# Twelve weight pages of block one multiplied in high and low halves, a first sum of squares that needs no constants from memory, and a fill moved

## The reference

```python
h = rms_norm(x, norm1_g[l])                     # divides by the root of the mean square over 1024
proj = h @ w_in[l]
p_rwkv, p_sb, q_mem, gate_logits = jnp.split(proj, cut, axis=-1)
...
q, k, v = jnp.split(p, 3, axis=-1)              # stick-breaking branch: v is h @ 512 columns
...
kv = rms_norm(mem, mem_g) @ w_kv                # memory branch
mk, mv = jnp.split(kv, 2, axis=-1)              # 512 columns of keys, 512 of values
```

## Time and profile before

| | us |
|---|---|
| median of 3 runs | 1359.57 |
| the profiled execution | 1355.61 |
| its span in the trace | 1353.8 |
| PE busy | 1259.5 (93%) |
| DVE busy | 818.7 (60%) |
| ACT busy | 680.1 (50%) |
| POOL busy | 571.1 (42%) |

### The profile page before, as it was taken

The page is one execution under the profiler, slowest core; times in us unless marked ns, Lnnn a source line. Parts: engine busy times, 40 slices in busy tenths (PEclk is TensorE's granted clock), DMA queues, the critical chain, the costliest instruction groups (busy, mean ns, idle before and its releaser), DMA issues.

```text
span 1353.8 us, 21687 instructions
## 1 busy us (share of the span) xinstructions
PE 1259.5 (93%) x8350; PEld 904.4 (67%) x8350; DVE 818.7 (60%) x1859; ACT 680.1 (50%) x1508; POOL 571.1 (42%) x385
## 2 busy tenths in 40 slices
PE   9999999999999999999999998888989888888786
PEld 7988988989999999987896443333434333433232
DVE  5876003473478763467247777666677676667755
ACT  4832233745676665653335654445554445554544
POOL 1100043327888888720014444444444444444342
PEclk9999999999999999999999999999999999999999
DMA  7433232335555555555739999999999999999997
GB/s 267 139 112 97 95 109 79 127 137 167 178 177 182 187 187 187 171 191 200 261 122 423 421 421 422 421 422 421 421 422 421 421 422 421 422 421 421 422 421 300
DMA packets 67935, 381.02 MB, mean 281 GB/s; under 512 B 7552, under 2 KB 7552, under 8 KB 35200
## 3 DMA queue, kind: packets, MB, share of 16 engines
q0 software_dynamic: 37296, 268.45, 47.8%
q1 hardware_dynamic: 29664, 107.84, 23.8%
q10 hardware_dynamic: 880, 3.41, 0.6%
HBM read 378.63 MB, written 1.05 MB: 280 GB/s over the span
## 4 chain that ended last, share of the span: by engine, by line
PE 59%; DMA 27%; ACT 6%; DVE 5%; issue 2%; POOL 1%; SPq 0%; POOLq 0%; DVEq 0%; ACTq 0%
DMA arena_block<-in_experts,arena_block 26%; PE bank L467 23%; PE bank L1092 10%; PE bank L503 5%; PE bank L521 3%; PE bank L465 2%; DVE arena_block L2480 2%; PE bank L1016 2%; PE bank L889 2%; PE bank L1116 1%; PE bank L485 1%; DMA const<-in_const 1%; ACT arena_block L1702 1%; PE bank L1026 1%; PE bank L566 1%
## 5 line engine op out<-in xcount | busy, mean ns | idle before, releaser
L1092 PE MATMUL bank<-arena_block 128*128 128x512 f32 x1012 | 486.5, 611 | 82.1 <-ACT arena_block L1702 80.5
L2617 POOL DMA_INDIRECT arena_block<-in_experts,arena_block x253 | 273.7, 1082 | 466.4 <-PE bank L1092 331.5
L2480 DVE SCALAR_TENSOR_TENSOR arena_block<-arena_block 128x1024 f32<-128x1024 f32 x256 | 314.0, 1227 | 188.9 <-DMA arena_block<-in_experts,arena_block 184.9
L1092 PEld LDWEIGHTS bank<-arena_block 128*128 128x128 f32 x1012 | 178.4, 190 | 350.1 <-ACT arena_block L1702 212.2
L2594 POOL TENSOR_TENSOR w_lo<-ring,w_hi 128x1024 fp32r<-128x1024 f32 x100 | 242.8, 2450 | 85.0 <-ACT w_hi L1200 84.7
L1696 ACT ACTIVATE arena_block<-arena_block 128x1 f32<-128x1 f32 x256 | 75.1, 294 | 279.7 <-DVE arena_block L2480 279.4
L1200 ACT ACTIVATE w_hi<-ring 128x1024 fp32r<-128x1024 f32 x119 | 125.2, 1053 | 51.9 <-PE bank L503 28.8
L467 PE MATMUL bank<-x_hi,w_hi 128*128 128x256 f32 x384 | 109.0, 284 | 0.0
L467 PE MATMUL bank<-x_hi,w_lo 128*128 128x256 f32 x384 | 108.7, 283 | 0.0
L467 PE MATMUL bank<-x_lo,w_hi 128*128 128x256 f32 x384 | 108.7, 283 | 0.0
L1702 ACT ACTIVATE arena_block<-const,arena_block 128x128 f32<-128x128 f32 x256 | 102.7, 401 | 8.3
(11 more groups left out here) (537 smaller groups left out, 2418.0 us busy)
## 6 DMA issues: line engine op xcount, KB each, us to landing
ring<-in_pages SPq DMA_DIRECT2D x175, 512.0 KB, 3.4
wq_pages<-in_pages SPq DMA_DIRECT2D x16, 512.0 KB, 4.6
arena_block<-in_experts,arena_block POOLq DMA_INDIRECT x259, 14.9
arena_block<-in_pages SPq DMA_DIRECT2D x8, 512.0 KB, 6.9
arena_mix<-in_memT ACTq DMA_DIRECT2D x1, 1024.0 KB, 8.9
arena_block<-in_subkT ACTq DMA_DIRECT2D x1, 1024.0 KB, 6.3
const<-in_const SPq DMA_DIRECT2D x1, 974.5 KB, 13.1
out_tok<-arena_block SPq DMA_DIRECT2D x3, 256.0 KB, 7.4
```

The lines of the kernel that those rows point to most:

```text
L1092: last = mm(bank[2 * tt + j][:, :], diag[:, slot, :], uv[slot][:, D + j * 512:D + (j + 1) * 512], start=start, stop=stop)
L2480: stt(uv[s][:, 0:D], uv[s][:, 0:D], 1.0, htok[:, tt, :], ALU.mult, ALU.mult, accum_out=e_act[:, s:s + 1])\
L2617: nc.gpsimd.indirect_dma_start(out=uv[slot], out_offset=None, in_=A["experts"], in_offset=bass.IndirectOffsetOnAxis(ap=eidx[:, n:n + 1], a ...
```

## The change

Pages 26 to 37 become split pages (`SPLIT_END` from 26 to 38), so `sbv`, `mk` and `mv` are three fp32r products where they were one float32 product. ScalarE makes their high halves (`a_high(26)` to `a_high(37)`) and VectorE their low ones (`a_low(26)` to `a_low(37)`), in places of the arena that are free then (`value_hi`, `early_hi`, `mem_hi`). The normed memory is split as well (`memn_hi` on ScalarE, `memn_lo` on VectorE). Low halves of pages up to 37 are counted by a semaphore of their own, `lo_first`. The four squares of `sbq`, `sbk`, `mq` and `mk` on VectorE move behind the last page of `mv`. The fill of `DT` moves behind `a_low(26)`. The first sum of squares uses a tile of ones that VectorE writes at the start and stands behind page 1, outside any page; the wait for `const` moves to behind page 5.

```diff
-SHIFTED, ROWED, FIRST_SPLIT, SHIFTED_END, FROM_KEYS, SPLIT_END = 14, 5, 7, 17, 19, 26
+SHIFTED, ROWED, FIRST_SPLIT, SHIFTED_END, FROM_KEYS, SPLIT_END = 14, 5, 7, 17, 19, 38
...
         def page_ready(page):
-            if page in NTH:
-                pe.wait_ge(S("lo_ready"), NTH[page])
+            if page in FIRSTS:
+                pe.wait_ge(S("lo_first"), NTH[page])
+            elif page in NTH:
+                pe.wait_ge(S("lo_ready"), NTH[page] - LATER)
...
-        linear("in_a", xg, part=(2, 1), between=first_norm)
-        a_page(3, 3)
+        pe.wait_ge(S("warm_tile"), 2)
+        pe.wait_ge(S("sq_tree"), 3)
+        mm(bank[4][:, 0:T], hn[:, 1, 0:P], norm_at[0][0][:, 0, :], start=True, stop=True).then_inc(S("norm_sum"), 1)
+        a_page(2, 4)
+        pe.wait_ge(S("const_in"), 16)
...
-        linear("sbv", hn, by_token=True, part=(1, 1))
+        linear("sbv", hn_hi_first, hn_lo_early, by_token=True, part=(1, 1))
...
-        pe.wait_ge(S("norm_out"), 2)
-        linear("mk", memn, part=(0, 1))
+        pe.wait_ge(S("b_dve"), B_DVE["memn_split"])
+        linear("mk", memn_hi, memn_lo, part=(0, 1))
...
-        linear("mv", memn, by_token=True)
-        pe.wait_ge(S("hn_high"), 1)
+        linear("mv", memn_hi, memn_lo, by_token=True)
+        pe.wait_ge(S("b_act"), B_ACT["hn_high"])
...
         take("sbv", flat(sbv), part=(0, 1))
+        a_high(28)
         act.wait_ge(S("b_dve"), B_DVE["inv3"])
...
+        act.wait_ge(S("norm_out"), 2)
+        A_(memn_hi, memn, ACT.Copy).then_inc(S("b_act"), 1)
         take("sbv", flat(sbv), part=(1, 1))
+        a_high(29)
...
         v.memset(hn[:, 0, :], 0.0).then_inc(S("warm_tile"), 1)
+        v.memset(hn[:, 1, 0:P], 1.0).then_inc(S("warm_tile"), 1)
...
         near_cross(2)
-        dve.wait_ge(S("in_a_copy"), SHIFTED_END - SHIFTED)
-        v.memset(DT, 0.0)
...
         pairs_read(5)
-        dve.wait_ge(S("in_a_copy"), N_IN_A - SHIFTED - 4)
-        tt_(sq_of["sbq"], sbq, sbq, ALU.mult)
+        a_low(26)
+        v.memset(DT, 0.0)
         pairs_read(6)
+        a_low(27)
...
+        a_low(28)
+        dve.wait_ge(S("b_act"), B_ACT["memn_high"])
+        tt_(memn_lo, memn, memn_hi.bitcast(F32), ALU.subtract).then_inc(S("b_dve"), 1)
+        a_low(29)
```

More of the change, by code:

```diff
@@ L50 @@
 SPLIT = IN_PLACE + [p for p in range(SPLIT0, N_PAGES) if p not in WHOLE]
+LATER = len(FIRSTS)
 LAST_GATE = EARLY[15]
@@ L273, in build @@
     hn_hi_first = typed(9728, "hn_hi_first", KT)
+    value_hi = [typed(start, f"value_hi{i}", 4).rearrange("p a b -> p (a b)") for i, start in enumerate((W0 + 15640, W0 + 16664))]
+    mem_hi = [value_hi[0], typed(4096, "mem_hi", 4).rearrange("p a b -> p (a b)")]
+    memn_hi = typed(2048, "memn_hi", KT)
+    lo_space = nc.sbuf_tensor("memn_lo", [P, KT, T], F32R)
+    memn_lo = lo_space.__enter__()[:, :, :]
+    lo_space.__exit__(None, None, None)
     y_hi, y_lo = typed(18944, "y_hi", 8), typed(11776, "y_lo", 8)
@@ L286, in high_room @@
         if page in FIRSTS:
-            return first_hi[page % SLOTS if page < PAGE0["in_a"] + SHIFTED_END else page % 2]
+            if page < PAGE0["in_a"] + SHIFTED_END:
+                return first_hi[page % SLOTS]
+            if page < PAGE0["sbv"]:
+                return first_hi[page % 2]
+            if page < PAGE0["mk"]:
+                return value_hi[page % 2]
+            return early_hi[page % 2] if page < PAGE0["mv"] else mem_hi[page % 2]
         if page in EARLY:
@@ L402, in _ @@
             if page - SLOTS in NTH and page - SLOTS not in IN_PLACE:
-                sp.wait_ge(S("lo_ready"), NTH[page - SLOTS])
+                sp.wait_ge(S("lo_ready"), NTH[page - SLOTS] - LATER)
             else:
@@ L525, in norm_sum @@
         def norm_sum(i):
-            if i < 2:
-                pe.wait_ge(S("sq_tree"), 3 * i + 3)
+            if i == 1:
+                pe.wait_ge(S("sq_tree"), 6)
             else:
@@ L700, in _ @@
                 pe.wait_ge(S("norm_out"), 1)
-                linear("sbv", hn, by_token=True, part=(0, 1))
+                linear("sbv", hn_hi_first, hn_lo_early, by_token=True, part=(0, 1))
             near_dd(lv)
             pairs(2 * lv + 1)
-        linear("sbv", hn, by_token=True, part=(1, 1))
+        linear("sbv", hn_hi_first, hn_lo_early, by_token=True, part=(1, 1))
         pe.wait_ge(S("b_dve"), B_DVE["inv3"])
@@ L710, in _ @@
         last.then_inc(S("b_pe"), 1)
-        linear("sbv", hn, by_token=True, part=(2, 1))
+        linear("sbv", hn_hi_first, hn_lo_early, by_token=True, part=(2, 1))
         pe.wait_ge(S("b_act"), B_ACT["pp32"])
@@ L719, in _ @@
         last.then_inc(S("b_pe"), 1)
-        linear("sbv", hn, by_token=True, part=(3, 1))
+        linear("sbv", hn_hi_first, hn_lo_early, by_token=True, part=(3, 1))
         pe.wait_ge(S("b_dve"), B_DVE["dd32"])
@@ L731, in _ @@
         last.then_inc(S("b_pe"), 1)
-        linear("mk", memn, part=(1, 1))
+        linear("mk", memn_hi, memn_lo, part=(1, 1))
         pe.wait_ge(S("b_dve"), B_DVE["pairs7"])
         chunk_g(0)
-        linear("mk", memn, part=(2, 1))
+        linear("mk", memn_hi, memn_lo, part=(2, 1))
         pe.wait_ge(S("b_act"), B_ACT["dd64"])
         chunk_u(0)
-        linear("mk", memn, part=(3, 1))
+        linear("mk", memn_hi, memn_lo, part=(3, 1))
         chunk_y(0)
@@ L1346, in _ @@
         act.wait_ge(S("norm_out"), 1)
-        A_(hn_hi, hn, ACT.Copy).then_inc(S("hn_high"), 1)
+        A_(hn_hi, hn, ACT.Copy).then_inc(S("b_act"), 1)
         take("mk", mk, part=(0, 1))
+        a_high(32)
         act.wait_ge(S("b_pe"), B_PE["dd64"])
@@ L1368, in _ @@
         take("mk", mk, part=(1, 1))
+        a_high(33)
         g_copy(0)
         take("mk", mk, part=(2, 1))
+        a_high(34)
         u_copy(0)
         take("mk", mk, part=(3, 1))
+        a_high(35)
         y_copy(0)
-        take("mv", flat(mv), part=(0, 2))
+        take("mv", flat(mv), part=(0, 1))
+        a_high(36)
+        take("mv", flat(mv), part=(1, 1))
+        a_high(37)
         high(EARLY[0])
@@ L1867, in a_low @@
             dve.wait_ge(S("hi_ready"), NTH[page])
-            tt_(ring_lo[:, page % SLOTS, :], ring[:, page % SLOTS, :], high_room(page).bitcast(F32), ALU.subtract).then_inc(S("lo_ready"), 1)
+            tt_(ring_lo[:, page % SLOTS, :], ring[:, page % SLOTS, :], high_room(page).bitcast(F32), ALU.subtract).then_inc(S("lo_first"), 1)
         norm_mean(0)
@@ L1994, in _ @@
         step(tt_(col[:, 25:26], V("mem_q_g"), V("mem_k_g"), ALU.mult))
+        for b in range(30, 36):
+            a_low(b)
         dve.wait_ge(S("b_pe"), B_PE["state"])
@@ L1997, in _ @@
         tt_(S1, two(bank[4][:, 0:T], 64), fac.broadcast_to([P, 4, 64]), ALU.mult).then_inc(S("b_dve"), 1)
-        dve.wait_ge(S("mk_out"), N_MK)
+        a_low(36)
+        a_low(37)
+        dve.wait_ge(S("mv_out"), N_MV)
+        tt_(sq_of["sbq"], sbq, sbq, ALU.mult)
+        tt_(sq_of["sbk"], sbk, sbk, ALU.mult)
+        tt_(sq_of["mq"], mq, mq, ALU.mult)
         tt_(sq_of["mk"], mk, mk, ALU.mult).then_inc(S("b_dve"), 1)
```

14 lines of the change are left out of this document (5 added, 9 removed).

## The result

| | before | after |
|---|---|---|
| median of 7 runs each, us | 1358.63 (1354.34 to 1362.05) | 1366.72 (1364.78 to 1368.86) |
| the profiled execution, us | 1355.61 | 1366.72 |
| its span, us | 1353.8 | 1364.9 |

The ratio of the runs is 1.0057, with a 95% interval of 1.0038 to 1.0075: some 8 us slower. The two profiled executions differ by 11.1 us. The forecast was +9.7 us, between the two.

The account below looks back on a forecast made before the run. Block one was taken to be bound by TensorE's own time. Terms +13.0 (by-token pages), -2.1 (`mk`) and -1.2 (first sum) gave +9.7 us, on the median 1359.57 forecast as 1369.3; own range 1365 to 1376, overall 1352 to 1379.

Parts of the forecast that it names:

- By-token pages: `sbv` and `mv`: 48 instructions a page instead of 32, 0.109 us each, held by weight loads; +13.0 us together.
- `mk`: Four by-feature pages of the memory's keys, split: 3.05 us each, 12.2 against 14.32 us, so -2.1 us.
- First sum: Start of the kernel: the ones product moves behind page 1, page 5 starts at 24.8 instead of 26.0 us; -1.2 us.
- Halves at no cost: VectorE and ScalarE make the new halves before their pages are due, `a_low(26)` and `a_low(28)` being tightest; cost 0.
- Fill and squares: On VectorE: moving the `DT` fill gives nothing; the four squares are due over 20 us behind `mv`; 0.
- Not in the sum: TensorE waits in the first 215 us for nothing the profile shows: read as 0.9 us, given no term.
- The median: The summed +9.7 us was put on the median of the runs, 1359.57, giving 1369.3 us, 0.7% slower.
- slower by over 0.5%: Whole kernel: outcome given 0.75, 0.55 from the forecast and late halves, 0.20 from narrow products at float32's rate.
- Loads of a reduced type: Rival, by-token pages: loads hidden, 128-column products follow at 0.066 us; -6.8 us in all, 1352.8 us; 20%.
- A narrow product: Rival, by-token pages: a narrow fp32r product streams at float32's rate, 0.227 us each; +55 us, 1415 us; 20%.
- Halves were not late: Rival: TensorE waits for VectorE's halves at two to four new pages, 1.2 to 2 us each; +4, 1373 us; 10%.

Follow-up runs that it names:

- two_products: Changed kernel without the third product (low weights by high activations) on the eight by-token pages, so their values lack that term: 1353.45 us.
- paired: Changed kernel with by-token pages multiplied two at a time, 256 columns moving past each load: 1351.50 us, ratio 0.9951 to the kernel before.
- fill_back: Changed kernel with the fill of `DT` back in its old place, between the second and third pair product: 1367.50 us in one run.
- paired_fill: The kernel of paired with the fill of `DT` in its old place and `a_low(29)` ahead of the last inverse's step: 1348.94 us, ratio 0.9945 to before.
- after_again: Changed kernel, unaltered, measured once more beside paired_fill: 1369.57 us, ratio 1.0085 to the kernel before.
- narrow: Changed kernel with seven blocks of unused extra products of several widths behind the first page of `mv`: 1395.53 us.
- sum_only: Kernel before with only the first sum of squares and its tile of ones changed: 1353.84 us in one run.
- sum_only_timed: Same kernel as sum_only, timed in 12 runs: 1356.65 us against 1358.14 for the kernel before, ratio 0.9991.
- keys_only: Changed kernel with only the four `mk` pages in halves, `sbv` and `mv` whole as before: 1352.51 us, ratio 0.9958 to the kernel before.
- the narrow kernels: narrow and a second changed kernel with extra products, its blocks of 64 columns last and whole `mv` pages between: 1395.53 and 1387.72 us.

## Why the prediction was right

- **By-token pages, the term that decides.** Forecast 5.38 us a page and 21.1 for `mv`, +13.0; measured 5.50 and 21.59, +14.0. The mechanism held, the load of 128 stationary columns. The row it rested on, line 596 at 0.108 us for 64 float32 columns, was near, but the 0.109 taken from it was 3% low: a reduced product of 128 columns costs 0.112. Times 384 instructions that is the missing 1 us.
- **`mk`.** -2.1 forecast, -2.3 measured. The row was right; two pages cost 2.93 instead of 3.05.
- **First sum.** -1.2 forecast, -1.3 measured, page 5 at 24.75 as forecast at 24.8.
- **Halves at no cost.** No wait for a low half from page 26 on. The two tight ones were done 0.5 and 0.4 us later than I worked out, and the pages came later too. What hid them was the long page itself: in two_products and paired, with short pages, the low half before page 28 is on the chain.
- **Fill and squares.** Nothing in either place (fill_back). The squares stand at 192.6 to 201.6 us, and nobody waits for them. Two of them are 3.4 us long instead of 1.2, the two with low halves of GpSimd beside them (193.56 to 196.04 and 196.77 to 199.34). But "the fill gives nothing" holds for this kernel only; in paired_fill it is part of a move that takes away a wait of 0.9 us.
- **Not in the sum.** TensorE's stalls without a releaser, +0.8 us. I had them as 0.9 us in one row and left them as they were. The view behind the earlier trace rows has two rows more, 0.5 us without a releaser at line 589 and the 1.2 us for `h_norm` at the start, so the reading was 0.5 us short. After the change they are 2.8 us in all against some 2 before. The long one is 2.40 us in after, fill_back and after_again alike.
- **The median.** The forecast of 1369.3 was made on 1359.57; the two medians are 1366.72 and 1369.57. The terms in the trace sum to +11.2, the runs say +8 and +13. The clock's dips can account for part of that spread; the rest stays open. So the mechanism is borne out term by term, but that 9.7 lies so near the middle of 8 and 13 is partly luck: against the trace it is 1.5 us low. The forecast's own range, 1365 to 1376, is wider than the 0.107 to 0.120 us it names: by the same sum these give 1368.5 to 1373.5, and the first median, 1366.72, lies outside that. And "slower by over 0.5%" was met narrowly, at 0.57% with an interval from 0.38% in the first comparison, clearly in the second.
- **The rivals.** Loads of a reduced type are not hidden: 0.112 us, not 0.066. A narrow product does not stream at float32's rate: 0.112, not 0.227. Halves were not late. The Trainium skill, page FP8 and Floating Point Precision, section TensorE Precision Notes, gives true float32 four passes through the array, and of reduced float32 it says only that it is read and truncated; counted as one pass each, as the prediction did, three products would be cheaper, and it is so with 256 moving columns (3.07 against 3.65 us a page) but not with 128 (5.50 against 3.77).

## What to carry to other kernels

In these rows a TensorE product costs about the larger of its two sides, the weight load (set by the stationary columns) and the stream (set by the moving columns and the passes of the type). A split in high and low halves takes stream away and adds loads, so here it paid where 256 columns move past a load and lost where 128 do. Where it loses, first look for a second page that can move past the same load, and then count again what was hidden by the long products.

## What the runs showed of the hardware that was not expected

- **The granted clock fell behind a short run of small products.** In both kernels with a block of 128 stationary by 64 moving columns (32 and 16 products) the clock fell right behind it, from 1.00 to the lower level, 0.50, and a page of 48 products cost 10.22 us instead of 5.3. It fell there although TensorE was busy throughout. But in narrow it stayed at 1.00 behind 32 products of 64 by 64, and in every kernel here behind the 16 of line 596 (611 in after), which have the same size in float32. So not every block of small products brings it down; what does was not tried.
- **The granted clock dips in some executions of one program and not in others.** Over 40 to 60 us it was 1.00 in sum_only and 0.91 in sum_only_timed, the same kernel; within it, from 54.6 to 57.9 us, it was 0.50, the lower level, with TensorE busy throughout. The page there took 4.57 us instead of 3.07, so 1.5 us. The same dip stands at the same page in the profiles of after_again, keys_only, paired and two_products, and not in the seven others. Two profiles can differ by that much for no reason in the code.
- **Stalls of TensorE without a releaser.** The long one is always at about the same place, inside page 22 at 103 to 107 us: 0.88 us before, 2.40 in after, 1.9 and 2.1 in the narrow kernels, 1.17 in sum_only, 0.82 in keys_only, 1.55 and 1.27 in the paired kernels, none in two_products. The executions of after and fill_back agree on 2.40; sum_only gave 0.66 in its other profile. The record of DMA transfers has something that the waits don't show: a transfer of 16 KB on queue 8, of the kind "instruction", landed 1.1 to 1.5 us before each of these stalls ended. Some of them:

| | transfer, us | stall, us | from landing to end of stall |
|---|---|---|---|
| before | 102.38 to 104.01 | 104.25 to 105.13 | 1.1 |
| after | 103.20 to 104.16 | 102.98 to 105.38 | 1.2 |
| after_again | 104.52 to 105.48 | 104.49 to 106.89 | 1.4 |
| sum_only | 101.20 to 102.95 | 103.05 to 104.21 | 1.3 |
| paired | 103.47 to 104.71 | 104.57 to 106.12 | 1.4 |
| two_products | 102.05 to 103.01 | none, at 104.7 | |

Other transfers of this kind land with no stall behind them. The second stalls fit too (in after a landing at 108.13 and an end at 109.49, in before 107.67 and 108.97). In after the transfer starts only when TensorE has already stopped, in before it starts 1.9 us before TensorE stops. So TensorE seems to wait here for its own instructions, and the +0.8 us of the account would be a price of their arrival. That is a reading of the times; no run moved these transfers, and why one comes late is open.
